# Two passes instead of three for the scores of layer 1: both parts of one map's keys in one tile

## The reference

```python
s = jnp.einsum('bqhmd,bshmd->bhmqs', qb, k).astype(F32) * scale
p = jax.nn.softmax(s, axis=-1)
w = (p[:, :, 0] - lam * p[:, :, 1]).astype(v.dtype)
return jnp.einsum('bhqs,bshe->bqhe', w, v)
```

## Time and profile before

| | |
|---|---|
| median of 3 runs | 2682.21 us |
| profiled execution, whole time | 2676.47 us |
| its span, first to last instruction | 2674.8 us |
| its mean granted TensorE clock | 0.98 of full |
| scores' matmuls of 320 columns, both layers | 192 x 3 (first map and layer 0), 128 x 3 (second map) |
| heads of layer 1, first turn to last score | 1371.9 to 2378 us of the span |

### The profile page before, as it was taken

The page is one execution under the profiler, slowest core; times in us unless marked ns, Lnnn a source line. Parts: engine busy times, 40 slices in busy tenths (PEclk is TensorE's granted clock), DMA queues, the critical chain, the costliest instruction groups (busy, mean ns, idle before and its releaser), DMA issues.

```text
span 2674.8 us, 37846 instructions
## 1 busy us (share of the span) xinstructions
PE 2512.1 (94%) x12040; PEld 2028.3 (76%) x12040; DVE 1769.0 (66%) x3252; ACT 853.2 (32%) x1777; POOL 417.8 (16%) x473
## 2 busy tenths in 40 slices
PE   7899999998898899989999999999999999999996
PEld 3478877877777777867887887777877888877785
DVE  3745788878887546766446666666666666655776
ACT  4322223322222222223233333343334333332223
POOL 0000222211222010010032212222222211101000
PEclk9999999999999999989999999999999999999998
DMA  9745544444554465554432322232223333237556
GB/s 346 228 142 176 187 146 143 141 157 157 173 175 139 146 225 181 191 189 141 158 105 75 106 76 96 90 96 90 85 92 97 96 98 96 88 122 252 195 188 228
DMA packets 167004, 395.54 MB, mean 148 GB/s; under 512 B 15121, under 2 KB 15761, under 8 KB 162385
## 3 DMA queue, kind: packets, MB, share of 16 engines
q1 hardware_dynamic: 135104, 254.32, 30.0%
q0 software_dynamic: 31760, 139.48, 15.0%
HBM read 332.93 MB, written 63.18 MB: 148 GB/s over the span
## 4 chain that ended last, share of the span: by engine, by line
PE 55%; DVE 19%; DVEq 9%; issue 6%; DMA 5%; ACT 4%; POOLq 1%; POOL 1%; ACTq 0%; SPq 0%
PE ps L617 43%; DVE small L1161 3%; PE ps L524 3%; DVEq L1159 3%; PE ps L506 2%; PE ps L515 2%; DVE w_lo L1276 2%; DMA w_raw<-in_w_ada_dram 2%; DVEq L1299 1%; PE ps L604 1%; DVEq L1386 1%; DVE ada_sum L1306 1%; PE ps L633 1%; DVE small L1059 1%; DVE wT_lo L1153 1%
## 5 line engine op out<-in xcount | busy, mean ns | idle before, releaser
L617 PE MATMUL ps<-w_hi,hT_hi 128*128 128x512 f32 x2760 | 1123.7, 407 | 15.1 <-issue 7.5
L617 PE MATMUL ps<-w_hi,hT_lo 128*128 128x512 f32 x2760 | 1086.6, 394 | 0.0
L617 PE MATMUL ps<-w_lo,hT_hi 128*128 128x512 f32 x2760 | 1082.0, 392 | 0.0
L617 PEld LDWEIGHTS ps<-w_hi,hT_lo 128*128 128x128 f32 x2760 | 520.7, 189 | 115.5
L617 PEld LDWEIGHTS ps<-w_hi,hT_hi 128*128 128x128 f32 x2760 | 524.1, 190 | 108.0 <-issue 13.3
L1276 DVE TENSOR_TENSOR w_lo<-w_raw,w_hi 128x512 fp32r<-128x512 f32 x560 | 404.2, 723 | 294.6 <-ACT w_hi L871 285.4
L617 PEld LDWEIGHTS ps<-w_lo,hT_hi 128*128 128x128 f32 x2760 | 523.2, 190 | 89.3 <-issue 1.4
L871 ACT CAST w_hi<-w_raw 128x512 fp32r<-128x512 f32 x560 | 345.7, 620 | 468.3 <-PE ps L617 454.5
L1306 DVE SCALAR_TENSOR_TENSOR ada_sum<-w_raw,cond,ada_sum 128x512 f32<-128x512 f32 x480 | 366.6, 805 | 32.3 <-issue 8.9
L816 ACT ACTIVATE work<-ps,small 128x640 f32<-128x640 f32 (+1 forms) x120 | 85.2, 710 | 356.8 <-DVE small L1164 356.8
L1161 DVE TENSOR_REDUCE small<-ps 128x1 f32<-128x640 f32 (+1 forms) x200 | 143.6, 718 | 59.9 <-PE ps L515 42.0
(11 more groups left out here) (205 smaller groups left out, 2649.7 us busy)
## 6 DMA issues: line engine op xcount, KB each, us to landing
w_raw<-in_w_in_dram SPq DMA_DIRECT2D x216, 512.0 KB, 3.8
w_raw<-in_w_ada_dram SPq DMA_DIRECT2D x256, 256.0 KB, 2.9
z<-stage POOLq DMA_DIRECT2D x27, 1280.0 KB, 5.2
w_raw<-in_w_out_dram SPq DMA_DIRECT2D x64, 512.0 KB, 4.2
work<-z POOLq DMA_DIRECT2D x72, 320.0 KB, 3.8
w_raw<-in_w_ada_dram SPq DMA_DIRECT2D x44, 512.0 KB, 5.0
work<-o POOLq DMA_DIRECT2D x8, 1280.0 KB, 7.4
x<-stage POOLq DMA_DIRECT2D x7, 1280.0 KB, 8.1
```

The lines of the kernel that those rows point to most:

```text
L617: last = nc.tensor.matmul(ps[:, t, :], x[:, kt, t * P:(t + 1) * P], w[:, kt % RING, :], start=(kt == 0 and i == 0), stop=(kt == KT - 1 and ...
```

## The change

In layer 1 the two parts of one map's keys stand in one tile: `kT[0]` has the first map's high part in partitions 0 to 63 and its low part in 64 to 127, `kT[1]` the second map's low part in 0 to 63 and its high part in 64 to 127. The query's high part stands twice, in both halves of `qT[0]` (first map) and `q_low[0]` (second map); its low part stands beside the high keys, with zeros opposite. One pass is then high by high plus high by low, and a second low by high. Layer 0 is as before.

```diff
-AT1 = [0, 1, 2, 8, 12, 16, 20, 24, 28, 30, 32, 34, 36, 38, 40, 41, 43, 44, 46, 49, 51, 53, 55, 56, 58, 59]
+AT1 = [0, 1, 2, 9, 13, 17, 21, 25, 29, 30, 32, 34, 36, 38, 40, 41, 43, 44, 46, 49, 51, 53, 55, 56, 58, 59]
...
 # TensorE, scores
-                q_of = q_low if n % L.maps == 1 else qT
+                m = n % L.maps
+                if L.maps == 1:
+                    passes = ((qT[0], kT[0]), (qT[0], kT[1]), (qT[1], kT[0]))
+                else:
+                    passes = tuple((x, kT[m]) for x in (qT, q_low)[m])
...
-                    for i, (x, y) in enumerate(((0, 0), (0, 1), (1, 0))):
-                        last = nc.tensor.matmul(ps[:, SC + b, 0:w], q_of[x][:, q0:q0 + P],
-                                                kT[y][:, k0:k0 + w], start=(i == 0), stop=(i == 2))
+                    for i, (x, y) in enumerate(passes):
+                        last = nc.tensor.matmul(ps[:, SC + b, 0:w], x[:, q0:q0 + P], y[:, k0:k0 + w],
+                                                start=(i == 0), stop=(i == len(passes) - 1))
...
 # ScalarE, turn
-                    r0, r1 = rows or (0, P)
-                    last = nc.scalar.copy(dst[r0:r1, :], ps[r0:r1, turn_bank(r), c0:c1])
+                    r0, r1, to = rows or (0, P, 0)
+                    last = nc.scalar.copy(dst[to:to + r1 - r0, :], ps[r0:r1, turn_bank(r), c0:c1])
...
 # ScalarE, pieces of layer 1
+                q_pieces = [[((c0 % 512, c0 % 512 + c1 - c0), (qT, q_low)[m][0][:, c0:c1], 64 * m, 64 * m + 64, 64 * to)
+                             for m in range(2) for to in (m, 1 - m)] for c0, c1 in ((0, 512), (512, 640))]
+                k_pieces = [[(at, kT[m][:, c0:c1], 64 * m, 64 * m + 64, 64 * m) for m in range(2)]
+                            for at, c0, c1 in (((0, 512), 0, 512), ((128, 384), 512, 768))]
...
 # VectorE, pieces of layer 1
+                q_pieces = [[((c0 % 512, c0 % 512 + c1 - c0), z[0][:, c0:c1], z[1][:, c0:c1], 64 * m, 64 * m + 64, 64 * m)
+                             for m, z in enumerate((qT, q_low))] for c0, c1 in ((0, 512), (512, 640))]
+                k_pieces = [[(at, kT[m][:, c0:c1], kT[m][:, c0:c1], 64 * m, 64 * m + 64, 64 * (1 - m)) for m in range(2)]
+                            for at, c0, c1 in (((0, 512), 0, 512), ((128, 384), 512, 768))]
...
 # VectorE, once ahead of the heads
-            for n in range(2):
-                nc.vector.memset(qT[n][64:P, :].bitcast(F32), 0.0)
-                nc.vector.memset(q_low[n][0:64, :].bitcast(F32), 0.0)
+            nc.vector.memset(qT[1][64:P, :].bitcast(F32), 0.0)
+            nc.vector.memset(q_low[1][0:64, :].bitcast(F32), 0.0)
```

More of the change, by code:

```diff
@@ L830, in attention_act @@
                 q_pieces = [[((c0 % 512, c0 % 512 + c1 - c0), qT[0][:, c0:c1])] for c0, c1 in ((0, 512), (512, 640))]
+                k_pieces = [[((0, 512), kT[0][:, 0:512])], [((128, 384), kT[0][:, 512:768])]]
             else:
[L832 to L836, removed]
+                q_pieces = [[((c0 % 512, c0 % 512 + c1 - c0), (qT, q_low)[m][0][:, c0:c1], 64 * m, 64 * m + 64, 64 * to)
+                             for m in range(2) for to in (m, 1 - m)] for c0, c1 in ((0, 512), (512, 640))]
+                k_pieces = [[(at, kT[m][:, c0:c1], 64 * m, 64 * m + 64, 64 * m) for m in range(2)]
+                            for at, c0, c1 in (((0, 512), 0, 512), ((128, 384), 512, 768))]
+            pieces = ([q_pieces[0], k_pieces[0], q_pieces[1] + k_pieces[1]]
                       + w_pieces + w_pieces + [[((0, P), wT[0][:, 0, 0:P])]])
@@ L1151, in turn @@
                 for (c0, c1), hi, lo, *rows in pieces:
-                    r0, r1 = rows or (0, P)
-                    last_op = nc.vector.tensor_tensor(lo[r0:r1, :], ps[r0:r1, turn_bank(r), c0:c1],
+                    r0, r1, to = rows or (0, P, 0)
+                    last_op = nc.vector.tensor_tensor(lo[to:to + r1 - r0, :], ps[r0:r1, turn_bank(r), c0:c1],
                                                       hi[r0:r1, :].bitcast(F32), ALU.subtract)
@@ L1212, in attention_dve @@
                             for c0, c1 in ((0, 512), (512, 640))]
-            else:
[L1214 to L1218, removed]
+                k_pieces = [[((0, 512), kT[0][:, 0:512], kT[1][:, 0:512])],
+                            [((128, 384), kT[0][:, 512:768], kT[1][:, 512:768])]]
+            else:
+                q_pieces = [[((c0 % 512, c0 % 512 + c1 - c0), z[0][:, c0:c1], z[1][:, c0:c1], 64 * m, 64 * m + 64, 64 * m)
+                             for m, z in enumerate((qT, q_low))] for c0, c1 in ((0, 512), (512, 640))]
+                k_pieces = [[(at, kT[m][:, c0:c1], kT[m][:, c0:c1], 64 * m, 64 * m + 64, 64 * (1 - m)) for m in range(2)]
+                            for at, c0, c1 in (((0, 512), 0, 512), ((128, 384), 512, 768))]
+            pieces = ([q_pieces[0], k_pieces[0], q_pieces[1] + k_pieces[1]]
                       + w_pieces + w_pieces + [[((0, P), wT[0][:, 0, 0:P], wT[1][:, 0, 0:P])]])
```

## The result

The changed kernel takes 2714.46 us (median of 4 runs, 2709.28 to 2720.53) against 2682.26 for the one before (2681.81 to 2686.22): ratio 1.0118, 95% interval 1.0094 to 1.0141. It is slower, as forecast, but by 32 us where 14.4 were predicted, and half a us above the range.

A forecast was written before the change was run, and what follows sets the result against it. VectorE's and ScalarE's chain, not TensorE, was taken to bound layer 1's heads up to S6. Nine heads at +1.8, +0.4, +0.85 and -3 made +14.4 us: 2697 us, own range 2688 to 2710, full range 2682 to 2714.

The forecast's parts named there:

- the chain ahead of S0: First turn (T0) to first score (S0): added casts and low parts of k lengthen a chain without slack, +2.3 us a head.
- R3 to R5: Fourth to sixth wide-score maximum: moved slots put a weight tile's split between S3 and S4, +0.5 us a head.
- Rival A: TensorE bounds the kernel, so removing the pass gains 40 us, giving 2642; chance 0.12 (any gain above 0.2%).
- the step from S0 to R3: First score to fourth maximum: rotation starts with S0, combine saves 1.04, weight split pays 0.6; -0.4 us a head.
- The +0.6 that I gave as the upper bound: First score to fourth maximum: upper bound on the change per head, the lower being -1.0 us.
- Rival B: Rotation leaves VectorE's chain from S0: one combine and two small instructions save about 1 us each; 2682, chance 0.16.
- Rival D: Everything at its upper bound, casts of 0.80 and rotation +0.6: 3.3 us per head, 2712 in all; chance 0.12.
- S6 to the next T0: Seventh score to next head's first turn: TensorE is late, so shorter scores give -0.6 us a head (bounds 0.5 and 0.76).
- the three heads that I set apart: Layer 1's first head +0.4 us, the two behind the loop's jump +0.85 us for both.
- The last heads: Four heads of 80 slots, with more TensorE work between scores and slack ahead of S0: -3 us for the four.

The follow-up runs named there:

- edit 2: Changed kernel with ScalarE signalling turn 0 after two casts and making the query's second copies afterwards from SBUF: 2682.6 us, 1.0006.
- 1: Changed kernel with AT1's old slots, S0 to S5 one slot earlier again: 2705.0 us, ratio 1.0094 to the kernel before.
- 5: Kernel before the change with only AT1's new slots: 2684.0 us, ratio 1.0020.
- 7: Kernel before the change without its second pass in layer 1, nothing added: 2668.2 us, ratio 0.9967.
- 4: Changed kernel with the low pass issued twice in layer 1, so three passes again: 2722.0 us, ratio 1.0142 to the kernel before.
- 3: Late rotation: changed kernel with GpSimd's rotation of the next head moved behind the seventh score's exponential: 2689.7 us, ratio 1.0034 to the kernel before.
- 6: Late rotation in the kernel before the change: GpSimd's rotation moved behind the seventh score's exponential, three passes kept: 2665.6 us, ratio 0.9953.
- 9: Changed kernel with GpSimd's rotation held back until the first score's matmuls have ended: 2696.0 us, ratio 1.0053 to the kernel before.

## Why the prediction was wrong

**Right: that the chain ahead of S0 sets the head.** +2.42 against +2.3, of which edit 2 took off 1.0 with two casts; S0 waits for k's low part and not for its slot (1). R3 to R5 gave +0.50, and 5 shows it with three passes. Rival A is refuted from both sides: 40 us of matmuls are worth 11.6 us taken from the kernel before (7) and 7.6 put back into the changed one (4).

**Wrong: the step from S0 to R3, "I take -0.4", +0.38 measured.** I reasoned that a rotation that starts with S0 "ends before the first combine", and it does. I took its cost as a stretch that slides out of the chain, and charged one weight split for the other end. But the combine was not the only instruction held before. VectorE, seventh head before, three instructions that take 0.17 alone:

```profile
1750.32 1.04 DVE L1055 TENSOR_TENSOR small<-small 128x5 f32<-128x5 f32 x1
1751.44 0.61 DVE L1057 SCALAR_TENSOR_TENSOR small<-small 128x5 f32<-128x5 f32 x1
...
1755.09 1.12 DVE L1059 SCALAR_TENSOR_TENSOR small<-small 128x5 f32<-128x5 f32 x1
```

With the start at S0 the rotation also meets the two integer instructions, 1.45 us together in the seventh head, and often L1133. They stand ahead of R0: 1.66 us a head in the nine, none before. Against their lengths in 3 and 6, VectorE's instructions from S0 to R3 run 4.08 us a head longer after and 3.63 before: the combine's part left, and more came in.

Over the late rotation S0 to R3 pays 2.42 us after and 1.30 before, so the rotation costs 1.12 more. Without it S0 to R3 is 0.74 shorter after (11.80 against 12.54), and +0.38 is the difference. The cost is not monotone in the start. It is least at 1.2 to 1.6 us behind S0 among the starts tried (table under 9); before stood at 2.22, and the change moved past the least to the other side. The +0.6 that I gave as the upper bound held the measured value, so the bounds were right and the value chosen was not. Rival B named this contention and guessed its sign wrong; nor does its sum add up as written, since three instructions at about 1 us each are -3 and not -2.0. Rival D's 3.3 a head and 2712 are close to the 3.23 and 2714 by luck: its casts of 0.80 took 0.58.

**Wrong: S6 to the next T0, -0.6 predicted, -0.08 measured.** In the seven heads with no jump behind them it is -0.25, as much as the pass taken out alone gives there (7). S6 to S7 is 0.26 shorter; S7 to S8 stays at 3.9 (3.89 to 3.91), with two passes or three, so the second wide score gave nothing. S9 to the next T0 is 0.13 shorter in the seven heads, and S8 to S9 grows by 0.3 in the third, seventh and eleventh. I allowed for S8 waiting on VectorE, but took that to cost 0.16 of the 0.76. Why S7 to S8 does not move I can't say: TensorE stands still for only 0.07 us ahead of S8.

**Wrong: the three heads that I set apart.** The first and the two behind the loop's jump were given +1.25 together and lost 7.5. The first lost 4.2 where I had +0.4: S0 came 2.42 later as in the others, its rotation came 3.7 us behind S0, where it was 8.0 before, and its S0 to R3 went from 12.07 to 14.35. The other two carry their rotation 0.22 and 1.66 us behind S0 and take 15.04 and 12.85: the same effect inside one profile. The last heads gave less too: three of them won 1.4 together, where -3 stood for four (the fourth lies outside the 35.1).

Together: 9 x 1.43 = 12.9, 6.2 and 1.6 make the 20.7 between the +14.4 of the sum and the +35.1 of the heads. About half of it lies from S0 to R3 (9 x 0.78 = 7.0, and 3.2 in the three heads), where the rotation is, which I priced with a single row.

## What to carry to other kernels

Removing TensorE work pays only where TensorE is late: price it stretch by stretch, and price what the rearrangement adds to the chain that feeds it. Where an engine shares something with another, a shift of one against the other is an edit in itself: list every instruction that the new overlap meets, ahead of the old place as well as behind it. Here moving GpSimd's rotation out of the way, one call moved behind one wait, gained 14 us with three passes (6), and removing the pass by itself 12 (7).

## What the runs showed that I had not expected

- Instructions with one SBUF input that I saw held up beside GpSimd's rotation had five columns. A 128x5 int32 instruction took up to 1.26 us, 0.17 alone, and a 128x5 float one (L1133) 0.90 to 1.26 in the six heads where the rotation started ahead of S0. A 128x1 float one (L1169) kept 0.15 throughout, and the maxima out of PSUM never were held up. So the number type does not decide.
- The edge is sharp: in 2, the second integer instruction began 0.53 to 0.54 us behind S0 in eight of the nine typical heads. It took 1.26 us in the one where the rotation had begun 0.48 us behind S0, and 0.17 us in the seven where it began at 0.56 us or later.
- ScalarE's copy of a high part from SBUF to the other 64 partitions took 0.62 us against 0.58 out of PSUM.
